# When weight chunks are split beside the tiles of the preceding piece, in both input projections

## What is computed

```python
def _ab_project(h, w_in, pos):                      # layer 0: 2304 columns
    qa, ka, va, qb, kb, vb = jnp.split(h @ w_in, AB_SPLITS, axis=-1)
    qa, ka = _rope(qa...), _rope(ka...)             # va and vb are not rotated
    qb, kb = _rope(qb...), _rope(kb...)

def _c_project(h, w_in, b_f):                       # layer 1: 3088 columns
    q, k, v, f = jnp.split(h @ w_in, (C_W, 2 * C_W, 3 * C_W), axis=-1)
    logf = jax.nn.log_sigmoid(f + b_f)
...
    logf_all = jnp.concatenate([c_logf, logf], axis=1)   # 2048 rows of the cache, then 16 new ones
    c_all = jnp.cumsum(logf_all, axis=1)
```

## Time and profile before

| | us |
|---|---|
| median of 3 runs | 3993.86 (3986.52 to 3995.69) |
| profiled execution | 3993.36, its span 3991.6 |
| PE busy | 3572.8 (90% of the span) |
| DVE busy | 1687.2 (42%) |
| ACT busy | 1247.8 (31%) |
| mean granted clock of PE | 0.952 |

### The profile page before, as it was taken

One profiled execution on the slowest core, in us unless ns is written; L12 is line 12 of the kernel. 1 busy time (PEld: TensorE's weight loads), 2 busy tenths in 40 slices (PEclk: granted clock), 3 DMA queues, 4 the chain that ended last, 5 costly groups with the idle time before them and its releaser, 6 DMA issues. The chain is left out here.

```text
span 3991.6 us, 63233 instructions
## 1 busy us (share of the span) xinstructions
PE 3572.8 (90%) x23365; PEld 3123.3 (78%) x23365; DVE 1687.2 (42%) x3085; ACT 1247.8 (31%) x2296; POOL 260.8 (7%) x340
## 2 busy tenths in 40 slices
PE   7996795879799999997899899888889799999997
PEld 6776683658799999996789788655557799999997
DVE  4217783445333333335121388644444233333334
ACT  3215451444211111113221366445543211111111
POOL 2210000003100000004000000000002200000003
PEclk9997895989899999998999999999999899999999
DMA  4225424973211111112552343499974311111102
GB/s 147 77 94 120 96 59 149 372 266 111 80 53 42 32 53 42 32 42 85 134 152 92 86 109 89 130 352 342 347 256 172 95 32 53 42 32 53 42 21 100
DMA packets 379193, 466.99 MB, mean 117 GB/s; under 512 B 87136, under 2 KB 234352, under 8 KB 378544
## 3 DMA queue, kind: packets, MB, share of 16 engines
q1 hardware_dynamic: 379072, 465.39, 37.0%
HBM read 395.43 MB, written 70.80 MB: 117 GB/s over the span
## 5 line engine op out<-in xcount | busy, mean ns | idle before, releaser
L2155 DVE TENSOR_TENSOR f_gated<-f_gated,f_up 128x384 f32<-128x384 f32 x132 | 73.2, 554 | 740.9 <-ACT f_gated L2088 740.9
L2254 PE MATMUL f_gate<-m_ht_hi,f_w_hi 128*128 128x384 f32 x1056 | 355.1, 336 | 25.8 <-DVE f_w_lo L2147 25.8
L2179 DVE TENSOR_TENSOR f_y<-f_y,f_down 128x512 f32<-128x512 f32 x396 | 269.7, 687 | 229.8 <-PE f_down L2267 229.7
L2254 PE MATMUL f_gate<-m_ht_hi,f_w_lo 128*128 128x384 f32 x1056 | 354.6, 336 | 0.0
L2254 PE MATMUL f_gate<-m_ht_lo,f_w_hi 128*128 128x384 f32 x1056 | 354.6, 336 | 0.0
L2254 PE MATMUL f_up<-m_ht_hi,f_w_lo 128*128 128x384 f32 x1056 | 352.7, 334 | 0.0
L2254 PE MATMUL f_up<-m_ht_hi,f_w_hi 128*128 128x384 f32 x1056 | 352.7, 334 | 0.0
L2254 PE MATMUL f_up<-m_ht_lo,f_w_hi 128*128 128x384 f32 x1056 | 352.7, 334 | 0.0
L2267 PE MATMUL f_down<-f_wo_hi,f_act_hi 128*128 128x512 f32 x792 | 313.5, 396 | 10.7 <-DVE f_y L2179 9.3
L2267 PE MATMUL f_down<-f_wo_lo,f_act_hi 128*128 128x512 f32 x792 | 310.0, 391 | 0.0
L2267 PE MATMUL f_down<-f_wo_hi,f_act_lo 128*128 128x512 f32 x792 | 309.8, 391 | 0.0
(11 more groups left out here) (393 smaller groups left out, 7371.1 us busy)
## 6 DMA issues: line engine op xcount, KB each, us to landing
sc_kc<-in_cache_c_k SPq DMA_DIRECT2D x64, 1024.0 KB, 14.6
sc_vc<-in_cache_c_v SPq DMA_DIRECT2D x64, 1024.0 KB, 9.6
f_raw<-in_w_ffn_in SPq DMA_DIRECT2D x88, 512.0 KB, 5.0
sb_kc<-in_cache_b_k SPq DMA_DIRECT2D x32, 1024.0 KB, 13.9
sb_vc<-in_cache_b_v SPq DMA_DIRECT2D x32, 1024.0 KB, 12.2
f_raw_o<-in_w_ffn_out SPq DMA_DIRECT2D x22, 1024.0 KB, 6.4
f_raw<-x SPq DMA_DIRECT2D x18, 512.0 KB, 4.1
abp_raw<-in_w_ab_in SPq DMA_DIRECT2D x32, 256.0 KB, 2.9
```

Source lines behind the costliest of these rows:

```text
L2155: dve.tensor_tensor(prod[:, b], silu[:, b], up[:, q, 0:gw], ALU.mult).then_inc(prod_done, 1)
L2179: dve.tensor_tensor(part, part, down[:, half, :], ALU.add).then_inc(added, 1)
L2254: last = pe.matmul(acc[:, q, 0:gw], a[:, s, k, u, :], b[:, k, token], start=(k == 0 and j == 0), stop=(k == KT - 1 and j == 2))
```

## The change

Three things are changed. A new helper `split_at(c, t)` in each projection says which chunks of the next piece are split (ACT, DVE) and reloaded (SP) in the step of tile t of piece c: in the first piece none in tiles 0 to 3 and two in each of tiles 4 to 7, in every later piece chunk t in tile t, 0 to 7, and none in tile 8. In `project_ab` the split of the first piece's chunks is written ahead of the squares of tile 1 on ACT and ahead of the scaling of tile 0 on DVE. And `past_at` goes from 2 to `TILES + 3`, which is 12, tile 3 of the second piece of `project_c`. No instruction on tensors is added or taken away.

```diff
--- before.py
+++ after.py
@@ -140,6 +140,13 @@
         def heads_of(ap):
             return ap.rearrange("p (h d) -> p h d", d=DH)
 
+        def split_at(c, t):
+            if c + 1 == len(AB_PIECES):
+                return []
+            if c == 0:
+                return [2 * (t - 4), 2 * (t - 4) + 1] if 4 <= t < KT else []
+            return [t] if t < KT else []
+
         def value_stores(s):
             c, t = steps[s]
             if AB_TURNED[c] == AB_PIECES[c][1]:
@@ -192,8 +199,9 @@
                     sp.wait_ge(rot_done, s + 1)
                 for dst, src in key_stores(s):
                     sp.dma_start(dst, src).then_inc(k_stored[s % 2], 16)
-                if t >= 1 and c + 2 < len(AB_PIECES):
-                    load_w(c + 2, t - 1)
+                if c + 2 < len(AB_PIECES):
+                    for k in split_at(c, t):
+                        load_w(c + 2, k)
                 if 3 <= s < roped + 3:
                     r = s - 3
                     cr, tr = steps[r]
@@ -279,7 +287,7 @@
             for i in range(len(steps) + 4):
                 if i < TILES:
                     square(i)
-                if i == 1:
+                if i == 0:
                     for k in range(KT):
                         split_high(0, k)
                 if 2 <= i < TILES + 2:
@@ -290,8 +298,8 @@
                     evacuate(s)
                     if 3 <= s < roped + 3:
                         columns_out(s - 3)
-                    if t >= 1 and c + 1 < len(AB_PIECES):
-                        split_high(c + 1, t - 1)
+                    for k in split_at(c, t):
+                        split_high(c + 1, k)
 
         @block.vector
         def _(dve):
@@ -330,11 +338,11 @@
 
             dve.wait_ge(g_loaded, 16)
             for i in range(1, len(steps) + 4):
-                if i <= TILES:
-                    scale_h(i - 1)
                 if i == 1:
                     for k in range(KT):
                         split_low(0, k)
+                if i <= TILES:
+                    scale_h(i - 1)
                 if 2 <= i < TILES + 2:
                     low(i - 2)
                 if i == 4:
@@ -344,8 +352,8 @@
                     c, t = steps[s]
                     if s < roped:
                         rotate(s)
-                    if t >= 1 and c + 1 < len(AB_PIECES):
-                        split_low(c + 1, t - 1)
+                    for k in split_at(c, t):
+                        split_low(c + 1, k)
 
         @block.tensor
         def _(pe):
@@ -417,7 +425,7 @@
     n_v = 332
     w_v = w.rearrange("(k p) n -> p k n", p=P)
     q_v = qkt.rearrange("(j p) n -> p j n", p=P)
-    past_at, logf_at = 2, TILES + 5
+    past_at, logf_at = TILES + 3, TILES + 5
     with Stage(nc, name) as st:
         raw = st.sb("raw", [P, KT, wide])
         w_hi, w_lo = st.sb("w_hi", [P, 2, KT, wide], F32R), st.sb("w_lo", [P, 2, KT, wide], F32R)
@@ -441,6 +449,13 @@
              "b_loaded", "past_loaded", "zero_done", "f_done", "low_done", "soft_done", "logf_done", "past_turned",
              "past_copied", "prompt_turned", "prompt_done", "logf_stored", "new_loaded", "sample_done", "decay_stored"))
 
+        def split_at(c, r):
+            if c + 1 == len(C_PIECES):
+                return []
+            if c == 0:
+                return [2 * (r - 4), 2 * (r - 4) + 1] if 4 <= r < KT else []
+            return [r] if r < KT else []
+
         def row_stores(s):
             c, kind, t = steps[s]
             first, n, _ = C_PIECES[c]
@@ -489,8 +504,9 @@
                     sp.wait_ge(z_done, s + 1)
                     for dst, src in row_stores(s):
                         sp.dma_start(dst, src).then_inc(z_stored[s % 2], 16)
-                if 1 <= r <= KT and c + 2 < len(C_PIECES):
-                    load_w(c + 2, r - 1)
+                if c + 2 < len(C_PIECES):
+                    for k in split_at(c, r):
+                        load_w(c + 2, k)
                 if s - 2 in key_steps:
                     store_cols(s - 2)
                 if kind == "q":
@@ -563,8 +579,8 @@
                     evacuate(s)
                 if s - 2 in key_steps:
                     columns_out(s - 2)
-                if 1 <= r <= KT and c + 1 < len(C_PIECES):
-                    split_high(c + 1, r - 1)
+                for k in split_at(c, r):
+                    split_high(c + 1, k)
                 if s == TILES + 1:
                     act.wait_ge(low_done, 2)
                     act.activation(soft[:], zf[:], ACT.Exp).then_inc(soft_done, 1)
@@ -591,8 +607,8 @@
                 if kind == "f":
                     dve.wait_ge(z_done, s + 1)
                     dve.tensor_tensor(zf[:, r, :], z[:, s % 2, n_v:n_v + C_H], b[:], ALU.add).then_inc(f_done, 1)
-                if 1 <= r <= KT and c + 1 < len(C_PIECES):
-                    split_low(c + 1, r - 1)
+                for k in split_at(c, r):
+                    split_low(c + 1, k)
                 if past_at < s <= past_at + 4:
                     copy_past(s - past_at - 1)
                 if s == TILES:
```

## The result

The changed kernel takes 3952.06 us (median of 4 runs, 3951.05 to 3955.8) against 3994.78 (median of 4 runs, 3986.52 to 3998.94) for the kernel before; the ratio is 0.9897 (0.988 to 0.9915). It is taken over all runs; the two medians alone give 0.9893. Repeated later beside 15 runs of before it is 0.9906 (0.989 to 0.9922). Of all the runs of this document three single ones (4609.95, 5147.02 and 7084.9 us) were slow and count in no ratio. So the change saves 37 to 43 us, depending on whether one goes by the ratios or by the medians; 37.75 were forecast, and 3956 as the time. The profiled execution took 3951.05, with a span of 3949.3 against 3991.6.

The account below looks back on a forecast made before the run. PE, busy nine tenths of the span, bounds the kernel; only its idle or low-clock time in the projections can be gained. 21.1 + 11.4 + 2.75 + 2.5 = 37.75 us off 3993.36 gave 3956, range 3946 to 3967.

Parts of the forecast that it names:

- Ends of pieces in project_ab: Four piece ends in project_ab: waits of 14.2 us and low clock of 6.9 us behind them go, 21.1 us.
- Ends of pieces in project_c: Five piece ends in project_c: waits of 9.7 us and one clock fall of 1.7 us go, 11.4 us.
- First piece of project_ab: Start of project_ab: earlier scaling 1.85 us, splits gone before tiles 5 and 6 1.2, doubled splits cost 0.3; 2.75 us.
- First piece of project_c: Start of project_c: 7.39 us wait replaced by one before step 4, 4.2 us sooner, transposes return 1.7; net 2.5 us.
- (a): Rival in both projections: low clock isn't caused by the waits and stays, 6.9 + 1.7 us less gain, 3964.2; chance 0.11.
- (b): Rival at project_ab's piece ends: wait isn't for the split, or new order makes another; 3976.7; chance 0.04.
- (c): Rival in first pieces: project_ab's waits shrink more, or the store in project_c isn't what holds; 3948; chance 0.05.
- (d): Rival in both projections: slower, steps become longer everywhere, 0.7 us each over 72 steps; 4006; chance 0.02.
- (e): Rival in other stages: the shorter stages give the gain back elsewhere, within 8 us of before; chance 0.02.

Follow-up runs that it names:

- e5_filled: Kernel before, with PE's waits at the four ends of pieces in project_ab filled by matmuls whose result is overwritten; ratio 0.9971 to before.
- e7_one_per_tile: Changed kernel, but in project_ab's first piece one chunk is split per tile in tiles 0 to 7; ratio 0.9907 to the kernel before.
- e4_start_only: Kernel before, with only the start order changed: first piece's chunks split ahead of tile 1's squares and tile 0's scaling; ratio 0.9998.
- e3_past_only: Kernel before, with only the transposes of the cached decays moved to steps 12 to 15 of project_c; ratio 0.9997.
- e10_again: The changed kernel measured once more, in more rounds, with nothing altered; ratio 0.9906 to the kernel before.
- e6_past_spread: Changed kernel, with the eight loads of cached decays issued one per step in steps 0 to 7 of project_c; median 3946.86 us, ratio 0.9890 to before.

## Why the prediction was right

**Ends of pieces in project_ab.** Forecast 21.1 us, measured 21.0. Both parts came out: the waits, counted from start to start with 0.24 us more than the idle column, and the slow first steps as 6.9 us, which `e5_filled` gives alone. That the last digit agrees is partly luck: the five profiles with the old splits have AB 2-5 at 234.04 to 236.75, so another of them would have given 19.6 to 22.3 us. With two chunks split in tile 7 of the first piece it just fits, as reckoned, or rather misses by a tenth: the last split ends at 57.81 and the first matmul starts at 57.91. The same 0.1 us stands between them in all six profiles with the doubled splits, and 0.09 us stood between a split and the matmul that waited for it in the earlier trace rows. With one split per tile (`e7_one_per_tile`) the distance is 0.63 us, and the piece is 0.1 us shorter.

**Ends of pieces in project_c.** Forecast 11.4 us, less 1.7 for the transposes that come back there, so 9.7 for C 2-7; measured 9.9. Five waits at 0.2 us above the idle column were slightly too few: the lengths of the last four pieces concerned make it about 0.26. I had taken one fall of the clock for five waits, from the one profile that I had. Five profiles with the old splits show nine falls, 1.8 per execution, so on average 1.3 us more were to be had than the sum had. That the forecast and the measured pair of profiles agree here rests on the same profile of before, with its one fall, standing on both sides.

**First piece of project_ab.** Forecast 2.75 us, 4.1 between the two profiles, 3.4 between the means of five and four (61.1 and 57.7). This term was undersized. The start alone gives 2.6 (`e4_start_only`, one profile) where I had 1.85: the later issue of x(3) was rightly priced at nothing, but I had taken the loads behind it as shifting with tile 1, and x(5) came forward by 2.5 us. The splits taken from ahead of tiles 5 and 6 gave 1.25 where I had 1.2 (`e7_one_per_tile`), and the doubled ones cost 0.15 us of PE's time in one profile and none in the other, where I had 0.3. The mechanism is the one described, except for that extra shift, whose cause is open.

**First piece of project_c.** This step decided whether the 7.39 us of the earlier trace rows were to be had. Forecast: replaced by a wait before step 4, 4.2 us sooner. Measured: the wait is there, 4.93 us, and the piece is 4.9 us shorter, 4.8 in `e3_past_only`, but only 3.2 in `e10_again`; the means of the five old and six new profiles in which the loads stand in a row (38.1 and 33.3) are 4.8 apart. The slow step 4 took 5.50 where 5.76 were put in. The four groups cost 1.6 us in the second piece (it is 54.91 us long in the changed kernel, and the third, as wide and without them, 53.30), forecast 1.7.

**Rivals.** (a) is refuted in `project_ab` by `e5_filled`; in `project_c` the 35 ends without a wait and without a fall speak against it. (b) would have left 21 us; there is no wait at these ends. (c) is what happened in small (the first pieces gave 9.0 us gross where 7.0 were put in); its other half, that the store isn't what holds, is refuted by `e6_past_spread`. Of (d) there is no trace: AB 2-5 is the same to 0.1 us in all seven profiles with the new splits, and PE has no wait in it, so the chain that moved to tile 0 delays nothing. (e) is within scatter.

## What to carry over

Where the next block of operands is prepared one part per step, let the last part fall one step before the block is needed; the wait at each end looks small (2 to 4 us of 60), but the low clock behind it cost another 1.3 to 2.8 us in most cases here. Before pricing a wait, look for the next one that ends near it: here removing 7.4 us of waiting for a load gave 4.9, because a store queued behind the same row of loads held step 4. And a row of small loads ahead of the first stores on one queue should be dealt out over the steps.

## What was not expected of the hardware

- Waits of the same length are not always followed by the same clock: in `project_c` the clock fell behind the three waits of 1.8 to 2.0 us in 9 cases of 15 over five profiles with the old splits, and behind the two of 1.5 and 1.7 us in none of 10; in `project_ab` behind the wait of 2.2 us in 4 of 5, and behind the three of 3.7 us in all of 15.
- Eight loads of the cached decays (128 KB each in small pieces), issued in a row, held SP's queue for 13.5 us: the second took 5.7 us and the six behind it 1.0 to 1.4 us each; issued one per step they took 0.45 us each.
- The first 60 us of the program, with loads of x, of weights and the table all in flight, differ by up to 2.9 us between executions of the same code, while AB 2-5 repeats to 0.1 us with the new splits. With the old ones it varies by 2.7 us, with the falls of the clock.
